# Latent attention in a two-layer hybrid block: each item's weighing is issued one item later, with two buffers for the turned probabilities

## What is computed

```python
def blk(qb):
    s = jnp.einsum('bqhd,bkhd->bhqk', qb, k).astype(jnp.float32) * scale
    p = jax.nn.softmax(s, axis=-1).astype(v.dtype)
    return jnp.einsum('bhqk,bkhd->bqhd', p, v)
...
y_l = mla_attention(queries(zl, rope), jnp.concatenate([k_c, k_l], axis=1), jnp.concatenate([v_c, v_l], axis=1))
y_c = flat(mla_attention(queries(zc, None), k_c, v_c)) if need_ctx else None
```

## Time and profile before

| what | us |
|---|---|
| median of 3 runs (4060.85 to 4070.43) | 4064.53 |
| the profiled execution | 4066.41 |
| span of its instructions | 4064.2 |
| TensorE matmul busy | 3729.9 (92%) |
| TensorE weight load busy | 2561.3 (63%) |
| VectorE busy | 1091.3 (27%) |
| ScalarE busy | 706.7 (17%) |
| GpSimd busy | 127.7 (3%) |
| mean granted TensorE clock | 0.953 |

### The profile page before, as it was taken

One profiled execution on the slowest core, in us unless ns is written; L12 is line 12 of the kernel. 1 busy time (PEld: TensorE's weight loads), 2 busy tenths in 40 slices (PEclk: granted clock), 3 DMA queues, 4 the chain that ended last, 5 costly groups with the idle time before them and its releaser, 6 DMA issues.

```text
span 4064.2 us, 63166 instructions
## 1 busy us (share of the span) xinstructions
PE 3729.9 (92%) x26440; PEld 2561.3 (63%) x26440; DVE 1091.3 (27%) x2410; ACT 706.7 (17%) x1337; POOL 127.7 (3%) x184
## 2 busy tenths in 40 slices
PE   7999999998999999999999989998989998888886
PEld 3455775766776677777777755666667764444443
DVE  0322342425532411111110342324245241111111
ACT  3321322012212200000000332212022120010011
POOL 0000100000000000000000000100000000000000
PEclk9999999998989999999999999898979999999998
DMA  5570101010011289999999301110100229999997
GB/s 196 177 263 27 65 27 47 11 52 21 27 72 69 76 306 354 353 355 348 358 358 349 116 27 38 53 52 32 52 21 32 104 79 397 415 413 410 414 409 312
DMA packets 121756, 740.26 MB, mean 182 GB/s; under 512 B 7808, under 2 KB 13952, under 8 KB 84624
## 3 DMA queue, kind: packets, MB, share of 16 engines
q1 hardware_dynamic: 110000, 695.29, 43.7%
q0 software_dynamic: 11616, 43.05, 3.7%
HBM read 713.09 MB, written 25.21 MB: 182 GB/s over the span
## 4 chain that ended last, share of the span: by engine, by line
PE 75%; DMA 14%; DVE 6%; ACT 3%; issue 2%; DVEq 0%; SPq 0%; POOL 0%; ACTq 0%; POOLq 0%
PE psum L567 12%; PE psum L994 10%; PE psum L1021 9%; PE psum L495 7%; PE psum L488 5%; DMA ring<-in_w_e_down 5%; DMA ring<-in_w_e_gate 5%; PE psum L472 4%; PE psum L887 3%; PE psum L654 3%; DMA ring<-in_w_e_up 3%; PE psum L985 3%; PE psum L569 3%; PE psum L673 3%; PE psum L538 2%; PE psum L757 2%
## 5 line engine op out<-in xcount | busy, mean ns | idle before, releaser
L567 PE MATMUL psum<-HT,ring 128*128 128x256 f32 x2560 | 623.7, 400 | 17.9 <-DVEq L1603 7.8
L567 PEld LDWEIGHTS psum<-HT,ring 128*128 128x128 f32 x2560 | 508.9, 202 | 121.0 <-issue 28.5
L1021 PE MATMUL psum<-ring,work 128*96 128x512 f32 (+1 forms) x1408 | 467.7, 597 | 24.5 <-DMA ring<-in_w_e_down 24.2
L994 PE MATMUL psum<-work,ring 128*64 128x96 f32 x11264 | 473.9, 246 | 6.1 <-issue 4.7
L994 PEld LDWEIGHTS psum<-work,ring 128*64 128x64 f32 x11264 | 466.3, 137 | 20.3 <-issue 18.3
L985 PE MATMUL psum<-ring,work 128*64 128x256 f32 x1536 | 371.2, 399 | 102.9 <-DMA ring<-in_w_e_gate 74.0
L985 PEld LDWEIGHTS psum<-ring,work 128*64 128x64 f32 x1536 | 213.1, 143 | 236.2 <-DMA ring<-in_w_e_gate 89.3
L986 PE MATMUL psum<-ring,work 128*64 128x256 f32 (+1 forms) x1536 | 352.6, 369 | 0.0
L1021 PEld LDWEIGHTS psum<-ring,work 128*96 128x96 f32 (+1 forms) x1408 | 166.3, 150 | 290.5 <-issue 259.6
L1103 ACT ACTIVATE work<-psum,small 128x768 f32<-128x768 f32 (+3 forms) x176 | 131.1, 745 | 895.5 <-PE psum L1021 495.2
L495 PE MATMUL psum<-ring,HT 128*128 128x512 f32 (+1 forms) x768 | 276.0, 521 | 0.0
(11 more groups left out here) (173 smaller groups left out, 3390.9 us busy)
## 6 DMA issues: line engine op xcount, KB each, us to landing
ring<-in_w_e_gate SPq DMA_DIRECT2D x64, 2048.0 KB, 7.8
ring<-in_w_e_up SPq DMA_DIRECT2D x64, 2048.0 KB, 10.3
ring<-in_w_e_down SPq DMA_DIRECT2D x64, 2048.0 KB, 9.7
ring<-in_w_ada SPq DMA_DIRECT2D x24, 2048.0 KB, 7.9
ring<-in_w_e_gate SPq DMA_DIRECT2D x32, 1536.0 KB, 12.2
ring<-in_w_e_up SPq DMA_DIRECT2D x32, 1536.0 KB
ring<-in_w_e_down SPq DMA_DIRECT2D x32, 1536.0 KB
ring<-in_w_gate SPq DMA_DIRECT2D x16, 2048.0 KB, 8.7
```

Of the source, the lines that this page charges most:

```text
L567: pe.matmul(b[:, 0:256], w[:, k, d4 * P:(d4 + 1) * P], HT[:, k, off:off + 256], start=(k == 0), stop=(k == KD - 1))
L994: ins = pe.matmul(b[lo:lo + 64, f * cap:(f + 1) * cap], w[:, k, c0:c0 + 64], e_xs[:, k, 0:cap], start=(k == 0), stop=(k == KD - 1))
L1021: ins = pe.matmul(banks[6 + half][lo:lo + cap, :], e_hidT[:, at, 0:cap], w[:, k, half * 512:half * 512 + 512], start=(f == 0), stop=(f == ...
```

## The change

On TensorE, for latent attention only, the order becomes turn(i), scores(i+2), weigh(i-1); the last item's weighing follows the loop. The turned probabilities have two buffers, taken in turn (the second lies at column 15040 of the work area). weigh(i-1) waits for the copies of its own item alone, not for those of the item just turned. On VectorE the order becomes turned(i), maxima(i+2), result(i-1), combine(i+1), with maxima of the first two items ahead of the loop. In layer 1 the ring "d" has four banks (3, 4, 2, 5) where it had two; in layer 0 it keeps two, because the modulation work uses the others. Differential attention keeps its order and its single buffer.

```diff
--- before.py
+++ after.py
@@ -329,7 +329,7 @@
         a_tmp = area(o + 2 * NT * 384 + NT * 256 + NT * 32, 4 * 16 * 16)
 
         a_P = area(o, 2 * T).rearrange("p (b t) -> p b t", b=2)
-        a_PT = area(o + 2 * T, T)
+        a_PT = area(o + 2 * T, T), area(15040, T)
         a_y = area(o + 3 * T, NT * 256).rearrange("p (t c) -> p t c", t=NT)
         a_sc = area(o + 3 * T + NT * 256, NT * 256)
 
@@ -631,12 +631,16 @@
                     for off, n in SEG:
                         transpose_tiles("a", lambda t: a_ktm[:, t, h, :], seg_tiles(off, n), 96)
                 all_free("g")
-                ring("d", (3, 4))
-                ring("a", (2, 5))
+                if L == 0:
+                    ring("d", (3, 4))
+                    ring("a", (2, 5))
+                else:
+                    all_free("a")
+                    ring("d", (3, 4, 2, 5))
                 attention(L, [(h, t) for h in range(4) for t in QT], 1,
                           lambda it, m: a_qT[0:96, it[0], it[1] * P:(it[1] + 1) * P],
                           lambda it, m, off, n: a_kT[0:96, it[0], off:off + n],
-                          lambda it, b: a_P[:, b, :], a_PT, a_v)
+                          lambda it, b: a_P[:, b, :], lambda b: a_PT[b], a_v)
                 finish_transposes(a_y)
 
             def attention(L, items, maps, q, k, p, PT, v):
@@ -665,12 +669,12 @@
                         transpose_tiles("d", lambda t: p(it, i % 2)[:, t * P:(t + 1) * P], keys[first:first + 4])
                     marks[("T", L, maps, it)] = st["d"]
 
-                def weigh(it):
-                    pe.wait_ge(sems["d_free"], st["d"])
+                def weigh(i, it):
+                    pe.wait_ge(sems["d_free"], marks["T", L, maps, it])
                     b = job("d")
                     keys = range(sum(n for _, n in key_pieces(it[1])) // P)
                     for t in keys:
-                        ins = pe.matmul(b[:, 0:64], PT[:, t * P:(t + 1) * P], v[:, t, it[0], :],
+                        ins = pe.matmul(b[:, 0:64], PT(i % 2)[:, t * P:(t + 1) * P], v[:, t, it[0], :],
                                         start=(t == 0), stop=(t == len(keys) - 1))
                     ins.then_inc(sems["d_done"], 1)
 
@@ -686,18 +690,21 @@
                             scores(i + 1, items[i + 1])
                         turn(i, it)
                         merge_units(L, item_units(L, i))
-                        weigh(it)
+                        weigh(i, it)
                         continue
                     turn(i, it)
                     if i + 2 < len(items):
                         scores(i + 2, items[i + 2])
-                    weigh(it)
+                    if i > 0:
+                        weigh(i - 1, items[i - 1])
                     if L == 0:
                         q_ = ADA_FIRST + i
                         if q_ < ADA_ALL:
                             ada_rows(q_)
                         if ADA_FIRST < q_ <= ADA_ALL:
                             ada_turn(q_ - 1)
+                if maps == 1:
+                    weigh(len(items) - 1, items[-1])
                 pe.wait_ge(sems["s_free"], st["s"])
                 all_free("a")
                 all_free("d")
@@ -862,7 +869,7 @@
                     r = it[0] % 2 * 64
                     return d_k[r:r + 64, it[0] // 2, off:off + n]
 
-                attention(L, [(h, t) for h in range(4) for t in QT], 2, q, k, lambda it, b: d_P[:, b, 0, :], d_PT, d_v)
+                attention(L, [(h, t) for h in range(4) for t in QT], 2, q, k, lambda it, b: d_P[:, b, 0, :], lambda b: d_PT, d_v)
                 merge_units(L, DF_END)
                 finish_transposes(d_y)
 
@@ -1663,13 +1670,13 @@
                             ALU.mult, ALU.add)
                         dve.sem_inc(sems["att_a"], 1)
 
-                def turned(it):
+                def turned(i, it):
                     n = sum(n for _, n in key_pieces(it[1]))
                     for at in range(0, n, 512):
                         ln = min(512, n - at)
                         dve.wait_ge(sems["d_done"], c.nth("d_done"))
                         b = bank()
-                        copy(PT[:, at:at + ln], b[:, 0:ln])
+                        copy(PT(i % 2)[:, at:at + ln], b[:, 0:ln])
                         dve.sem_inc(sems["d_free"], 1)
 
                 def result(i, it):
@@ -1680,16 +1687,28 @@
                     dve.sem_inc(sems["d_free"], 1)
 
                 maxima(0, items[0])
+                if maps == 1:
+                    maxima(1, items[1])
                 combine(0, items[0])
                 for i, it in enumerate(items):
+                    if maps == 1:
+                        turned(i, it)
+                        if i + 2 < len(items):
+                            maxima(i + 2, items[i + 2])
+                        if i > 0:
+                            result(i - 1, items[i - 1])
+                        if i + 1 < len(items):
+                            combine(i + 1, items[i + 1])
+                        continue
                     if i + 1 < len(items):
                         maxima(i + 1, items[i + 1])
-                    turned(it)
+                    turned(i, it)
                     if i + 1 < len(items):
                         combine(i + 1, items[i + 1])
                     result(i, it)
-                    if maps == 2:
-                        merged(L, item_units(L, i))
+                    merged(L, item_units(L, i))
+                if maps == 1:
+                    result(len(items) - 1, items[-1])
 
             def head_norm(y, sc):
 
@@ -1749,7 +1768,7 @@
                 for t in first[1:] + [t for t in QT if t < CT]:
                     queries(t)
                 dve.sem_inc(sems["mla_rope"], 1)
-                attention(L, [(h, t) for h in range(4) for t in QT], 1, lambda b, m: a_P[:, b, :], a_PT, a_y, 96 ** -0.5)
+                attention(L, [(h, t) for h in range(4) for t in QT], 1, lambda b, m: a_P[:, b, :], lambda b: a_PT[b], a_y, 96 ** -0.5)
                 if L == 0:
                     dve.wait_ge(sems["mod"], 2)
                     modulation(0, 0, 16, 24)
@@ -1950,7 +1969,7 @@
                     rope(d_tm[:, t, :].rearrange("p (g c) -> p g c", c=32), t, 16, d_tmp)
                 dve.sem_inc(sems["mla_rope"], 1)
                 merged(L, DF_GAP)
-                attention(L, [(h, t) for h in range(4) for t in QT], 2, lambda b, m: d_P[:, b, m, :], d_PT, d_y, 32 ** -0.5)
+                attention(L, [(h, t) for h in range(4) for t in QT], 2, lambda b, m: d_P[:, b, m, :], lambda b: d_PT, d_y, 32 ** -0.5)
                 head_norm(d_y, d_sc)
                 finish(L, 3, d_y, pk("g_diff"), 1.0 - lam0, DF_END)
```

## The result

The changed kernel takes 4012.35 us (median of 4 runs, 4010.94 to 4016.5), the one before, over the four runs there now are of it, 4062.69: ratio 0.9878, interval 0.9857 to 0.9900. That is 50 us, or 41 to 58. Forecast were 4028 us and 37, so the sign and the main mechanism (the overlap) held and the size did not; the time lies under the range.

The account below looks back on a forecast made before the run. TensorE, busy 92%, was taken as the bound on average, but alternating with VectorE in latent attention. Gains 22.6 + 1.1 + 3.4 + 0.5 + 3.4 + 5.6 = 36.6 us off 4066.41, less 1.9 to the median: 4028 us, range 4018 to 4043.

Parts of the forecast that it names:

- Layer 1's overlap: Layer 1's latent attention: with the stalls gone an item takes 3.5 us, and the stage gains 22.6 us.
- It does not hold TensorE back: Layer 1: VectorE's cycle of 3.44 us fills 98% of a 3.5 us item, yet does not delay TensorE.
- VectorE becomes the bound: Rival, layer 1: VectorE's cycle is 4.1 us, 13 items lose 0.6, 8 us in all, so 4036; chance 0.15.
- Layer 0's waits: Layer 0: six waits before context queries shrink from 0.76 to about 0.2 us, gaining 3.4 us.
- The end: Layer 0's last three items, which have no modulation rows: last result at 313.2 instead of 316.60, 3.4 us gained.
- The clock: Less time at low clock: 5.6 us back at layer 0's head changes, 1.1 us behind layer 1's last result.
- my two thirds: Layer 0's head changes: of 8.5 us lost to low clock, two thirds, 5.6 us, come back.
- the 5 us either way: Allowance in the range for later stages meeting the clock at other moments and for runs differing by 10 us.
- The slower rival: Rival, both layers: the clock is not held, so the kernel is slower than before, 4066 to 4088; chance 0.03.

Follow-up runs that it names:

- the two halves: Two kernels against the kernel before: the new order in layer 1 alone, 4036.2 us, and in layer 0 alone, 4049.5 us.

## Why the prediction was right and where it was wrong

*Layer 1's overlap*: right in sum. 53.75 us from first turn to last result were worked out, 53.4 and 52.5 measured. Two errors cancelled. The item was put at 3.5 and is 3.24, then 3.33: turn 0.67, scores 1.29 and weighing 1.28 by the first item above, where I had 0.71, 1.36 and 1.48. The weighing loses most, and a likely reason is that its weights load ahead once no wait stands before it: the loads start at 2370.13, 0.22 ahead of the first matmul, where in the kernel before both started at 2384.56 (seen in the traces, not tested by a run of its own). At the stage's start and end more was lost than I had laid out: turn(14) to turn(15) took 3.33, not 2.1, since turn(15) waited 0.88 for its exponential. That the two errors cancelled is luck.

*"It does not hold TensorE back"*: wrong, as a step. VectorE's cycle was put at 3.44 and is 3.33 (reciprocal to copies takes 0.20, where I had 0.31), and it does bind the second half, by the path I had called slack, maximum to exponential to turn. Each item's lag of 0.09 adds up until the slack of two items is used. It costs under 1 us here, so the rival "VectorE becomes the bound" came true in kind and at a tenth of its price. In the changed kernel, too, the maximum and the next operation stand 0.03 apart (2369.06 + 0.96 to 2370.05), and the cycle closes at 3.33 with gaps of that kind. The drain that the Trainium skill, "VectorE: DVE Perf Modes", section "The DRAIN you can't avoid", puts behind each operation would have made it about 4.1: the trace does not agree. The same section lets an operation that it calls not held start earlier, a case that no run here separates.

*Layer 0's waits*: right in kind. 0.35 remained, not 0.2, but the six items of a head take 44.3 us at full clock where they took 45.5: 1.2 a head for 1.3 forecast. The end gained 3.6 for 3.4. One shift was left out of the sum: the end was laid out with weigh(20) in it, which has moved there from the stretch before. Turn(20) to turn(21) takes 3.47 us where it took 4.53, and at item 0 no weighing stands any more (0.5): 1.5 us that no term has.

*The clock*: this is the step that failed, in size and in place. I took 5.6 us for the falls at layer 0's head changes and 1.1 behind layer 1. I read one profile of before and priced the falls in it; they vary from run to run. At the head changes they cost 8.2, 3.3 and 6.6 us in three profiles of the old order, 6.0 in the mean, and nothing in the changed kernel's two, so there my two thirds came near by luck. Low clock between first turn and last result of layer 0 was 32.8, 20.6 and 27.4 us in the three, and 4.0 to 10.5 in nine of the new: some 20 us less, worth 10 (at a head change 6.8 us of low clock cost 3.3). About 3.5 of these lie at the end, where the 3.4 us forecast had them already, 6 at the head changes and 1 at the stage's start, where I had nothing. In layer 1 low clock was 5.4, 23.2 and 13.1 us against 0 to 0.7 in the profiles with the changed kernel's stage; the old stage took 78.2 us in the mean and not 76.3, which is 1.9 more inside the stage, where again I had nothing. Behind layer 1's last result nothing came back: 4.8 and 4.2 us of low clock in the two profiles of before, 3.4 and 6.8 in the two of the changed kernel. In all the clock gave about 9 us beyond what the other terms held, not 6.7. With the 1.5 left out and a layer 1 that is 0.9 shorter than laid out, that makes 41 us in the stages, 4 more than the 36.6 forecast.

*The rest.* The larger part of the miss is not in the stages. Between 41 and the medians' 48 to 50 us stand 7 to 9 that no stage shows. By means it is less: the nine timed runs of the changed kernel average 4015.3 us, the 44 of before 4061.0, 46 apart, and the two halves give 27.7 + 13.5 = 41. The timed runs of before spread over 27 us (4046 to 4074), and outside the stages profiles with either order lie between 3794 and 3813. So the 5 us either way that the range allowed for later stages and repeats were too few: the second step that failed. Whether part of the rest belongs to the change is open.

*The slower rival* had the sign of the clock wrong: the new order leaves TensorE fewer idle stretches, and in layer 0 the nine profiles with it and its short waits have 4.0 to 10.5 us of low clock, against 20.6 to 32.8.

## What to carry to other kernels

When an engine's wait is taken away, price the clock with it: at layer 0's head changes the falls of the clock around short waits cost this kernel 6.0 us, the waits themselves 3.6. Read the falls from several profiles of the kernel before, not from one. And where two engines' cycles lie within a few per cent, lay out the lag over all items, since a lag that adds up reaches the other engine in the end.

## What was not expected of the hardware

Adding 0.43 us of useless matmuls at six places of layer 0 (and more at its last two items and at each item of layer 1) made the kernel 7 to 9 us faster. A gap of 0.76 or 0.83 us ahead of a weighing was followed by a fall from 2.4 to 1.2 GHz at three, one, two and two of six places in the four profiles that have such gaps; a gap of 0.28 or 0.35 us at one place of 54 in nine profiles. The Trainium skill's "TensorE: Matmul & The Clock Gate", section "A second HAM failure mode: psum-queue depth-cycling", says that short idles between groups of matmuls can make the clock swing; here the trace agrees for layer 0. The round of four banks in layer 1, which I feared for, did no harm: low clock in that stage was at most 0.7 us in the five profiles with the changed kernel's layer 1, and nothing with two banks.
